# Token ranks for the first expert list: column sums of comparison tables on the tensor engine, and the context products in another order

## What is computed

```python
def ec_moe(h, router_w, w1, w3, w2):
    xt = h.reshape(B * T, D)
    cap = EC_FACTOR * (B * T) // N_EXPERTS
    aff = jax.nn.softmax((xt @ router_w).astype(jnp.float32), axis=-1)
    gate_vals, idx = lax.top_k(aff.T, cap)
    xe = xt[idx]
```

## Time and profile before

| | |
|---|---|
| time, median of 3 executions | 1676.25 us (1674.95 to 1676.91) |
| the profiled execution's own time | 1672.78 us |
| its span | 1671.0 us |
| PE busy | 1614.6 us (97%) |
| PE clock, mean granted share of full speed | 0.99 |
| first list: last tile's row made to first expert product | 843.5 to 858.7 us |

### The profile page before, as it was taken

The page is one execution under the profiler, slowest core; times in us unless marked ns, Lnnn a source line. Parts: engine busy times, 40 slices in busy tenths (PEclk is TensorE's granted clock), DMA queues, the critical chain, the costliest instruction groups (busy, mean ns, idle before and its releaser), DMA issues. The chain is left out here.

```text
span 1671.0 us, 28408 instructions
## 1 busy us (share of the span) xinstructions
PE 1614.6 (97%) x11328; PEld 1402.1 (84%) x11328; DVE 701.7 (42%) x1782; ACT 399.9 (24%) x965; POOL 359.4 (22%) x428
## 2 busy tenths in 40 slices
PE   5999999999999899899989999999999999999997
PEld 4876876666668666788879999999999999999995
DVE  4001146776655888222453322233332233333225
ACT  5220113341222476211221111111111111111114
POOL 2000000015323643111122111222211222221122
PEclk9899999999999999999999999999999999999999
DMA  8411212142212576323289888888888888888863
GB/s 321 131 58 44 68 34 57 39 126 31 53 38 86 172 210 226 114 78 114 79 307 362 301 295 275 287 294 275 316 291 292 276 298 282 285 315 290 288 215 128
DMA packets 213486, 323.75 MB, mean 194 GB/s; under 512 B 29680, under 2 KB 102377, under 8 KB 213371
## 3 DMA queue, kind: packets, MB, share of 16 engines
q1 hardware_dynamic: 180731, 282.66, 48.1%
q0 software_dynamic: 8560, 16.39, 5.1%
q10 hardware_dynamic: 24080, 23.02, 4.8%
HBM read 293.85 MB, written 24.99 MB: 191 GB/s over the span
## 5 line engine op out<-in xcount | busy, mean ns | idle before, releaser
L1843 PE MATMUL psum<-arena 128*128 128x144 f32 x4096 | 505.9, 286 | 2.1 <-DVE arena L2478 1.7
L1843 PEld LDWEIGHTS psum<-arena 128*128 128x128 f32 x4096 | 502.6, 190 | 3.2 <-ACT arena L1277 1.9
L1853 PE MATMUL psum<-arena 128*128 128x144 f32 x2048 | 253.5, 286 | 0.0
L1853 PEld LDWEIGHTS psum<-arena 128*128 128x128 f32 x2048 | 251.8, 190 | 0.0
L1430 PE MATMUL psum<-arena 128*128 128x384 f32 x720 | 243.5, 494 | 0.0
L2521 DVE TENSOR_TENSOR arena<-gt,psum 128x144 f32<-128x144 f32 x128 | 38.9, 304 | 443.0 <-PE psum L1843 361.6
L860 POOL DMA_INDIRECT expert_list<-gt x128 | 125.9, 983 | 456.2 <-DVE gt L2507 412.0
L1430 PEld LDWEIGHTS psum<-arena 128*128 128x128 f32 x720 | 134.8, 191 | 90.4 <-issue 3.4
L1433 PE MATMUL psum<-arena 128*128 128x256 f32 (+2 forms) x864 | 166.4, 353 | 0.0
L1433 PEld LDWEIGHTS psum<-arena 128*128 128x128 f32 x864 | 146.4, 193 | 18.3 <-issue 1.7
L2368 DVE SCALAR_TENSOR_TENSOR arena<-arena,gt 128x1024 f32<-128x1024 f32 x128 | 159.1, 1280 | 1.6 <-DMA arena<-affinity_rows 1.6
(11 more groups left out here) (356 smaller groups left out, 1619.0 us busy)
## 6 DMA issues: line engine op xcount, KB each, us to landing
arena<-in_exp_w SPq DMA_DIRECT2D x96, 2048.0 KB, 11.5
arena<-in_ada_w SPq DMA_DIRECT2D x24, 1024.0 KB, 7.0
arena<-in_w_in SPq DMA_DIRECT2D x11, 1024.0 KB, 5.5
arena<-in_x_sample SPq DMA_DIRECT2D x16, 512.0 KB, 4.3
arena<-affinity_rows SPq DMA_DIRECT2D x16, 512.0 KB
arena<-m_decay_rows ACTq DMA_DIRECT2D x36, 128.0 KB, 3.4
arena<-decay_rows ACTq DMA_DIRECT2D x24, 192.0 KB, 3.6
out<-arena SPq DMA_DIRECT2D x9, 512.0 KB
```

Source lines behind the costliest of these rows:

```text
L1843: ins = mm(bank[:, 0:SLOTS], w[:, k, col], xeT[:, k, :], start=(k == 0), stop=(k == KD - 1))
L1853: ins = mm(bk[4 + db % 2][:, 0:SLOTS], wslot[4 + db // 4][:, k, (db % 4) * P:(db % 4) * P + P], hid[:, k, :], start=(k == 0), stop=(k == K ...
```

## The change

- The two counts of the second part (tiles 5 and 6) and the wide one of the last tile now write their elementwise result, 128 partitions by 896 or 1024 columns of 0 and 1, into tables that are kept (`beats`).
- A column sum of such a table gives, for each token of an earlier tile, how many tokens of the table's tile it beats; 128 minus that is how many of them beat it. `beaten_by` (PE) makes each sum as a product of a 128 x 128 piece of the table with a column of ones, one column wide: ten for the first two tables (in `bk[1]`, pairs that accumulate) and seven for the last (in `bk[0]`).
- The twelve short counts (five of 256, seven of 128) and both joining additions go. In their place stand two additions of constants (384 for five tiles, 128 for two) and two subtractions of the sums.
- The one-hot of the last tile is made before the other seven, and its list product comes first.
- PE's order changes: of the eight context products one stands before the last table's sums, two behind them, and five behind the eight list products. One of three idle products behind the last router product goes.
- Semaphore counts follow.

```diff
--- before.py
+++ after.py
@@ -325,6 +325,7 @@
         list_ids = lists.bitcast(I32)
         icur = scrap(2).bitcast(I32)
         head_junk = view(R_S, 2, D)
+        beats = [view(o, NL * P) for o in (R_S + D, R_S, R_HT + NL * P)]
         y9, fgb, sq3 = view(0, NT, D), view(9216, D), view(10240, 2, D)
         nqT, nkT = view(R_M, 3, T), view(R_M + 3456, 3, T)
         nv = view(R_M + 6912, NT, 384)
@@ -402,7 +403,7 @@
         h2_full, h2_act, h2_dve, r_full = (sem(n) for n in ("h2_full", "h2_act", "h2_dve", "logits_full"))
         r_sub, r_act, r_aff, sel_full, k_done, k_cols = (sem(n) for n in (
             "r_sub", "router_act_done", "affinity_done", "selection_matmuls_full", "context_topk_done", "list_columns"))
-        hot_done, tokens_done, row_in = sem("one_hot_done"), sem("token_numbers_done"), sem("affinity_rows_moved")
+        hot_done, tokens_done, row_in = sem("comparisons_and_one_hots_done"), sem("token_numbers_done"), sem("affinity_rows_moved")
         ranks_set, list_sc, list_in = sem("e_ranks_set"), sem("e_list_scattered"), sem("e_list_in")
         rank_step = sem("e_rank_step")
         acc_init = sem("acc_holds_x1")
@@ -1268,7 +1269,7 @@
                 nc.scalar.activation(xcT[:, :, k, :], gathered(k).rearrange("p (e s) -> p e s", s=CAPC), ACT.Identity,
                                      scale=gs[1][:, k, 0:1], bias=modcol[:, 24 + k, 0:1])
             nc.scalar.activation(combT[:].rearrange("p a b -> p (a b)"), bk[1][:, 0:2 * P], ACT.Copy).then_inc(cx_act, 1)
-            act.wait_ge(sel_full, 8)
+            act.wait_ge(sel_full, 10)
             nc.scalar.activation(affT[0:NE + 2, :], psum[0:NE + 2, 2048:3072], ACT.Copy).then_inc(r_act, 1)
 
 
@@ -1790,23 +1791,48 @@
             idle_products(2)
             router_quarters(NT - 1)
             router(NT - 1)
-            idle_products(3)
-
+            idle_products(2)
+
+            def beaten_by(n, j, start, stop):
+
+                return mm(bk[1 if n < 2 else 0][:, 320 + j:321 + j], beats[n][:, j * P:j * P + P], ones[:, 0:1],
+                          start=start, stop=stop)
+
+            pe.wait_ge(hot_done, 2)
+            for j in range(3):
+                beaten_by(0, j, True, False)
+                beaten_by(1, j, False, True)
             pe.wait_ge(r_aff, 4)
             first_row(range(NT - 1, NT))
+            for j in range(3, NL - 3):
+                beaten_by(0, j, True, False)
+                ins = beaten_by(1, j, False, True)
+            ins.then_inc(sel_full, 1)
             pe.wait_ge(wo_mul, NT)
             pe.wait_ge(h2_dve, NT)
-            for k in range(KD):
-                ins = mm(gathered(k), x1[:, 0, k * P:k * P + P], gather_c, start=True, stop=True)
-                if k == KD // 2 - 1:
-                    ins.then_inc(cx_full, 1)
+
+            def gather_context(first, end):
+
+                for k in range(first, end):
+                    ins = mm(gathered(k), x1[:, 0, k * P:k * P + P], gather_c, start=True, stop=True)
+                return ins
+
+            gather_context(0, 1)
+            pe.wait_ge(hot_done, 3)
+            for j in range(NL - 1):
+                ins = beaten_by(2, j, True, True)
+            ins.then_inc(sel_full, 1)
+            gather_context(1, 3)
+            for n in range(NL):
+                c = (n - 1) % NL
+                pe.wait_ge(hot_done, 4 + n)
+                ins = mm(bk[3][:, 0:2], onehot[:, c, :], pair0[:, c, :], start=(n == 0), stop=(n == NL - 1))
+            ins.then_inc(sel_full, 1)
+            gather_context(3, KD // 2).then_inc(cx_full, 1)
+            gather_context(KD // 2, KD)
             for b in range(2):
                 ins = nc.tensor.transpose(bk[1][:, b * P:b * P + P], combine_c[:, b * P:b * P + P], ident[:])
             ins.then_inc(cx_full, 1)
-            for c in range(NL):
-                pe.wait_ge(hot_done, c + 1)
-                ins = mm(bk[3][:, 0:2], onehot[:, c, :], pair0[:, c, :], start=(c == 0), stop=(c == NL - 1))
-            ins.then_inc(sel_full, 1)
             pe.wait_ge(cx_act, 1)
             pe.wait_ge(r_aff, 5)
             for i in range(1, NT):
@@ -2445,26 +2471,31 @@
                     dve.wait_ge(sel_full, 4)
                     for c in range(E1):
                         first_count(0, E1, c, rank_a)
+                    dve.wait_ge(dve_step, steps[0])
+                    link(v.tensor_scalar(rank_a[:, 0:E1], rank_a[:, 0:E1], float((NL - E1) * P), None, ALU.add))
             softmax(3, 1 + E1, 1 + E2)
             h2_turned(NT - 1)
             dve.wait_ge(sel_full, 5)
-            for c in range(E1):
-                first_count(E1, E2, c, rank_b)
-            for c in range(E1, E2):
-                first_count(0, E2, c, rank_a)
-            v.tensor_tensor(rank_a[:, 0:E1], rank_a[:, 0:E1], rank_b[:, 0:E1], ALU.add)
+            for n, c in enumerate(range(E1, E2)):
+                count(beats[n][:, 0:E2 * P], psum[:, 3072:3072 + E2 * P], 0, aff[:, 1 + c, 0:1], c, rank_a[:, c:c + 1])\
+                    .then_inc(hot_done, 1)
             softmax(4, NT - 1, NT)
             dve.wait_ge(r_aff, 4)
             v.tensor_copy(pair0[:, :, 1], aff[:, 1:NT, 0])
             v.tensor_copy(aff[:, 1:NT, NE:NE + 2], aff[:, 1:NT, NE - 1:NE].to_broadcast([P, NL, 2])).then_inc(r_aff, 1)
+            dve.wait_ge(hot_done, 2)
+            link(v.tensor_scalar(rank_a[:, E1:E2], rank_a[:, E1:E2], float((NL - E2) * P), None, ALU.add))
             dve.wait_ge(sel_full, 6)
+            count(beats[2], psum[:, 3072:4096], 0, aff[:, NL, 0:1], NL - 1, rank[:, NL - 1:NL]).then_inc(hot_done, 1)
+            dve.wait_ge(hot_done, 3)
+            v.tensor_scalar(onehot[:, NL - 1, :], iota0, rank[:, NL - 1:NL], None, ALU.is_equal).then_inc(hot_done, 1)
+            dve.wait_ge(sel_full, 7)
+            link(v.scalar_tensor_tensor(rank_a[:, 0:E1], bk[1][:, 320:320 + E1], -1.0, rank_a[:, 0:E1], ALU.mult, ALU.add))
+            dve.wait_ge(sel_full, 8)
+            link(v.scalar_tensor_tensor(rank[:, 0:E2], bk[0][:, 320:320 + E2], -1.0, rank_a[:, 0:E2], ALU.mult, ALU.add))
             for c in range(NL - 1):
-                count(junk0[:, 0, c * P:c * P + P], psum[:, 3072 + (NL - 1) * P:4096], NL - 1, aff[:, 1 + c, 0:1], c, rank[:, c:c + 1])
-            link(count(junk0[:, 1], psum[:, 3072:4096], 0, aff[:, NL, 0:1], NL - 1, rank[:, NL - 1:NL]))
-            link(v.tensor_tensor(rank[:, 0:NL - 1], rank[:, 0:NL - 1], rank_a[:, 0:NL - 1], ALU.add))
-            for c in range(NL):
                 v.tensor_scalar(onehot[:, c, :], iota0, rank[:, c:c + 1], None, ALU.is_equal).then_inc(hot_done, 1)
-            dve.wait_ge(sel_full, 7)
+            dve.wait_ge(sel_full, 9)
             v.tensor_copy(icur[:, 0:1], bk[3][:, 0:1])
             v.tensor_copy(list_ids[:, 0:1], bk[3][:, 0:1])
             v.tensor_scalar(lists[:, 1:2], bk[3][:, 1:2], 1.0 / BIG, None, ALU.mult).then_inc(k_cols, 1)
```

## The result

| | before | changed |
|---|---|---|
| median of 5 executions | 1676.25 us (1674.95 to 1678.80) | 1683.21 us (1681.78 to 1683.82) |
| ratio to before | | 1.0044, 95% interval 1.0033 to 1.0055 |
| the profiled execution's span | 1671.0 us | 1681.1 us |
| one stage: start of the last router product to turning of the second gather | 838.88 to 891.81: 52.9 us | 840.72 to 901.79: 61.1 us |

A forecast was written before the change was run, and what follows sets the result against it. The expert phase was taken to pass its start on one to one, set by the first gather and PE's queue together. At half clock the affinities turn 6.7 us later: 1676.25 + 6.7 = 1683.0 us, range 1677.0 to 1687.0.

The forecast's parts named there:

- The forecast case: PE's clock falls at about 843.6 us, staying at 0.50 until well into the five context products; +6.7 us, chance 0.66.
- the sum of 6.7: At half clock the affinities are turned at 857.8 us, 6.7 us later than at 851.14.
- the second fall: PE's clock drops again in its 2.2 us wait for ACT behind the context transposes; up to 3 us more, near +10.
- The clock's return: Of five context products behind the list, about three run at half clock, some 3 us, and two at full; end 855.1.
- Nothing is late there now: Expert 0's later weight loads shift with the affinities and keep their distance to the products; waiting there is 2.1 us.
- The clock that holds: With no PE idle stretch over 0.3 us before 850, the clock stays up; +1.2, 1677.5 us, chance 0.28.
- the filled gap: Sums replace PE's idle 2.3 us before its last row product; a stretch at half clock there cost 1.7 us.
- the rival's sum: At full clock the affinities are turned at 852.35 us, 1.2 us later than at 851.14.
- Faster: Filling PE's 2.3 us gap saves clock losses of the usual execution; 1674.0 us, 2.3 below the median, chance 0.06.

The follow-up runs named there:

- noidle: The changed kernel with one idle product instead of nine ahead of the turning of the gathered rows; 1682.19 us, ratio 1.0044.
- fill: The kernel before with eight idle products instead of three behind the last router product; 1675.12 us, ratio 0.9997.
- early: The wide kernel with affinities turned before the list products, seven context products behind the list and four idle products instead of nine; 1672.19 us, ratio 0.9987.
- wideidle4: The wide kernel with four idle products instead of nine; 1676.69 us, ratio 1.0010.
- wide: The changed kernel with its 17 sums and eight list products made 128 columns wide, same order; 1674.47 us, ratio 0.9992.
- sumswide: The changed kernel with only the 17 sums made 128 columns wide, list products left at two columns; 1675.05 us, ratio 1.0002.
- order: The changed kernel with the eight context products and two transposes back ahead of the list products, sums one column wide; 1678.56 us, ratio 1.0018.
- earlynarrow: The early kernel with sums one column and list products two columns wide; 1676.06 us, ratio 1.0000.
- early8: The early kernel with eight idle products instead of four ahead of the turning of the gathered rows; 1671.80 us, ratio 0.9986.

## Why the prediction was right

**The forecast case came.** The clock fell near 843.6 (843.3), sums and list products ran at half clock, and it came back only in the five context products. The list was to be read 0.9 us later than before and was 1.9 later; the affinities were to be turned 6.7 later and were 7.5, counted from the last router product; the first expert product was 9.1 later. At the end of the stage, the second gather, 8.1 us are lost in the profiles; in the medians 7.0. The 10.1 us between the two spans hold another 1.8 that were lost ahead of the stage, where the change does nothing. The remaining 1 us between profiles and medians is within what executions of one kernel differ by.

That the sum of 6.7 lies within 0.3 us of the measured 7.0 is in part luck. It left out 0.8 us of half clock ahead of the affinities and 1.6 us of the second fall, which the first expert product shows. Of these 9.1 us, 1.0 came back by the second gather; 0.7 of it because the kernel before stood still longer inside expert 0 (0.83 us for the gather against 0.59, and 0.43 us at 878.2).

**Prices.** A sum was to take 0.23 us at full clock and twice that at half: 0.234 (1.40 for six) and 0.43 (2.98 for seven). The Trainium skill's 25 ns for up to 64 columns (TensorE: Matmul & The Clock Gate, section Back-to-back issue gap) was not seen at either clock: at full clock an instruction took 0.117 us. Each such instruction brings a weight load of 128 columns, at one column as at 128; that the load sets its length is likely, but no run varies the load. That DVE's wide count would end 3.5 us earlier was right (3.4).

**The clock's return** was put in the fourth of the five context products, at about 854; it came at 857.0, 3 us later, but the products started later too, at 854.1 in place of 851.5, on a stage that lay 1.8 later. The fall came at the same time of the span and so earlier in the stage: the four sums and the first context product were already at half clock, which I had put at full. That is, in the main, the other 0.8 us.

**The second fall** was a bound and not part of the sum. It came, in the 2.3 us of waiting for ACT, and made the turning of the affinities and the nine idle products 6.4 us long in place of 4.77.

**A step that was wrong.** "Nothing is late there now": the kernel before waited 0.83 us for the second gather. I had read the waits of L1843 and not those of L1821. The gathers were said to meet PE's queue at the start of expert 0, and the expert phase to hand on a shift one to one; in truth the turning of the affinities sets the second gather, and noidle shows that an earlier start of expert 0 alone gains nothing. It made little difference to the forecast, since the affinities and the first expert product both moved later in this change (7.5 and 9.1 us), but noidle's expectation failed by it.

**The rivals.** The clock that holds: the filled gap did not hold it. The Trainium skill's sentence that the gate follows how busy the PE has been (same page, section What's actually happening) does not cover this: PE was busy for 5.70 of 5.70 us from 843.3 and stayed at 1.2 GHz, and with the same instructions at 128 columns it stayed at 2.4 GHz. The kernel with wide products is the rival's case, and its affinities came 1.3 us later, as the rival's sum had it; its median did not (1.1 below the kernel before in place of 1.2 above). Faster: not seen, and with the filled gap in the kernel before (fill) no gain could be told. The measured 1683.2 lies in the range.

## What to carry to other kernels

Work moved to the tensor engine is priced with its clock, and not at the clock that stands in the trace of before: 17 products of one column, close together, were enough to bring it to half speed for themselves and for all that stood behind them, here for 13.7 us. Where a product takes no longer with more columns (here up to 128), make it wide; it cost 0.1 us for twelve instructions and was worth 8.7 us. And before trimming what stands ahead of a phase, look for the second thing that is awaited inside the phase; the first wait may be only as long as the second allows.

## What was not expected of the hardware

- The same 34 sum and 16 list instructions at 1 and 2 columns or at 128 columns: with the narrow ones the clock was at 0.50 from 843.3, for all but the first twelve sum instructions; with the wide ones it was at 1.00 throughout. The smaller work took the longer time.
- PE's clock fell in or behind waits of 2.0 to 3.6 us in the kernels before (2.33), changed (2.30), early (2.06), wideidle4 (2.88) and noidle (2.30 and 3.54), but not in wide, sumswide and wideidle4 where each waited 2.30 us for ACT with the clock at 1.00 before and after. In order it fell behind a wait of 0.61 us.
- The first gather of 512 KB took 4.4 to 4.7 us to land in the eight kernels without a load of that size at the same time, and 5.2 (earlynarrow), 5.9 (early8) and 6.3 us (early) where the affinity row's load was issued within about 1 us of it. The second gather, beside the weight loads, took 7.1 to 7.5 us.
